# A two-layer decoder trunk on one core: the first four tiles of each transition summed on TensorE from the old residual and y times a diagonal, and six constant products ahead of them

## The reference

```python
def rms_norm(x, g, eps=RMS_EPS):
    xf = x.astype(jnp.float32)
    y = xf * lax.rsqrt(jnp.mean(xf * xf, axis=-1, keepdims=True) + eps)
    return (y * g.astype(jnp.float32)).astype(x.dtype)
...
    h = x
    for i in range(DEPTH):
        hn = rms_norm(h, pre_mix_g[i])
        ...
            y = conformer_conv(hn, ...)      # layer 0
            y = diff_attention(hn, ...)      # layer 1
        h = h + rms_norm(y, post_mix_g[i])
        f = conv_ffn(rms_norm(h, pre_ffn_g[i]), ffn_w_in[i], ffn_w_dw[i], ffn_w_out[i])
        h = h + rms_norm(f, post_ffn_g[i])
        h = h + per_layer_embed(h, p[i], ple_pre_g[i], ple_w_gate[i], ple_b_gate[i],
                                ple_w_proj[i], ple_post_g[i])
    return h
```

## Time and profile before

| | |
|---|---|
| time, median of 3 runs | 2510.29 us (2509.94 to 2512.2) |
| the profiled execution's own time | 2504.14 us |
| its span in the profile | 2502.3 us |
| mean granted TensorE clock | 0.993 of full |
| PE busy | 2430.5 us, 97% of the span |
| DVE busy | 1666.5 us, 67% |
| ACT busy | 1307.0 us, 52% |

### The profile page before, as it was taken

How to read it: one execution, slowest core, us unless ns; L and a number is a source line. 1 busy time by engine, 2 the same in 40 slices (tenths; PEclk the granted TensorE clock), 3 DMA queues, 4 the chain that set the end, 5 groups by cost and what they waited for, 6 DMA issues and landing times.

```text
span 2502.3 us, 40724 instructions
## 1 busy us (share of the span) xinstructions
PE 2430.5 (97%) x12610; PEld 2082.6 (83%) x12610; DVE 1666.5 (67%) x2183; ACT 1307.0 (52%) x1882; POOL 27.6 (1%) x49
## 2 busy tenths in 40 slices
PE   7999899999999999999999999999999999999997
PEld 6888787888888888887788887888888888888876
DVE  5889756777777764446665577567777777544465
ACT  6555545555555544446454455465655656444463
POOL 1000000000000000000000000000000000000000
PEclk9999999999999999999999999999999999999999
DMA  6444254666566665555565543646666666655554
GB/s 212 133 133 135 76 192 153 193 186 188 183 190 194 192 202 194 193 193 200 183 181 188 189 155 128 203 148 191 194 192 187 185 185 198 204 193 194 194 197 138
DMA packets 365325, 448.28 MB, mean 179 GB/s; under 512 B 27084, under 2 KB 273726, under 8 KB 364076
## 3 DMA queue, kind: packets, MB, share of 16 engines
q1 hardware_dynamic: 363452, 436.75, 54.7%
q0 software_dynamic: 1776, 10.41, 1.3%
HBM read 444.95 MB, written 2.10 MB: 179 GB/s over the span
## 4 chain that ended last, share of the span: by engine, by line
PE 88%; issue 5%; DVE 3%; ACT 2%; DMA 1%; DVEq 0%; SPq 0%; POOL 0%; ACTq 0%; POOLq 0%
PE ps L1273 34%; PE ps L1275 17%; PE ps L1308 11%; PE ps L1310 11%; PE ps L1309 11%; PE ps L1346 2%; PE ps L1253 1%; DVE v_conv L935 1%; DMA gain<-in_post_ffn_g 1%; DVE w_lo L808 1%; PE ps L1412 0%; PE ps L1426 0%; DVE h L860 0%; ACT w_hi L503 0%; DVE x L843 0%
## 5 line engine op out<-in xcount | busy, mean ns | idle before, releaser
L808 DVE TENSOR_TENSOR w_lo<-raw,w_hi 128x1024 fp32r<-128x1024 f32 x824 | 1002.4, 1224 | 664.5 <-ACT w_hi L503 635.7
L1273 PE MATMUL ps<-x,w_hi 128*128 128x512 f32 x3840 | 1341.2, 394 | 7.0 <-DVE w_lo L808 3.8
L503 ACT CAST w_hi<-raw 128x1024 fp32r<-128x1024 f32 x824 | 859.4, 1049 | 839.7 <-PE ps L1275 423.4
L1275 PE MATMUL ps<-x,w_lo 128*128 128x256 f32 x3840 | 1073.7, 280 | 0.0
L1273 PEld LDWEIGHTS ps<-x,w_hi 128*128 128x128 f32 x3840 | 718.9, 187 | 169.8 <-DVE w_lo L808 5.0
L1275 PEld LDWEIGHTS ps<-x,w_lo 128*128 128x128 f32 x3840 | 724.9, 189 | 0.6
L1308 PE MATMUL ps<-w_hi,mid 128*128 128x512 f32 x704 | 274.1, 389 | 4.6 <-DVE w_lo L808 4.6
L1310 PE MATMUL ps<-w_hi,mid 128*128 128x512 f32 x704 | 273.9, 389 | 0.0
L1309 PE MATMUL ps<-w_lo,mid 128*128 128x512 f32 x704 | 273.9, 389 | 0.0
L1308 PE MATMUL ps<-w_hi,x 128*128 128x512 f32 x640 | 254.3, 397 | 7.0 <-DVE x L980 3.6
L1309 PE MATMUL ps<-w_lo,x 128*128 128x512 f32 x640 | 250.1, 391 | 0.0
(11 more groups left out here) (144 smaller groups left out, 1213.9 us busy)
## 6 DMA issues: line engine op xcount, KB each, us to landing
raw<-in_ffn_w_in SPq DMA_DIRECT2D x704, 256.0 KB, 3.1
raw<-in_ffn_w_out SPq DMA_DIRECT2D x352, 256.0 KB, 3.0
raw<-in_conv_w_pw SPq DMA_DIRECT2D x192, 256.0 KB, 3.1
raw<-in_attn_w_qkv SPq DMA_DIRECT2D x192, 256.0 KB, 2.9
raw<-in_ple_w_gate SPq DMA_DIRECT2D x128, 256.0 KB, 3.5
raw<-in_attn_w_o SPq DMA_DIRECT2D x64, 256.0 KB, 3.2
raw<-in_ple_w_proj SPq DMA_DIRECT2D x16, 256.0 KB, 3.4
h<-in_x SPq DMA_DIRECT2D x4, 512.0 KB, 5.9
```

What stands on the lines that cost most here:

```text
L503: nc.scalar.copy(w_hi[:, u % RING], raw[:, u % RING]).then_inc(hi_split, 1)
L808: nc.vector.tensor_tensor(w_lo[:, u % RING], raw[:, u % RING], w_hi[:, u % RING].bitcast(F32), ALU.subtract).then_inc(split_done, 1)
L1273: mm(ps[:, 4 * s + f], w_hi[:, u % RING, q, columns], x[:, kt].rearrange("p a t -> p (a t)"), start=kt == 0, stop=False)
L1275: ins = mm(ps[:, 4 * s + f, 0:T], w_lo[:, u % RING, q, columns], x[:, kt, 0], start=False, stop=kt == KT - 1)
```

## The change

The transitions are rebuilt. The gain products write `y` into SBUF (the place of `z`, at the arena's start) and no longer in place, so the eight PSUM banks are free sooner. The first four tiles of x (chunk 0 of h) no longer wait for the residual: PE sums each in PSUM from two ordinary products, old h times the identity and y times `rdiag`, the diagonal of rstd, which DVE makes. The residual for chunk 0 is done last. The other 12 tiles are transposed as before, four at a time, after units 0, 1 and 2 of the next stage. Ahead of the old-h products stand six products of constants (ones times identity, `keep_warm`), whose result nobody reads. The stage may start when two tiles of x are ready, not four (and not eight for the rest). The statistic of y is summed in two steps, with the first three chunks ahead. In the down stages the gains of chunks 0 to 2 are applied in the last chunk. The tile slots in PSUM are now 8 to 15 (banks 4 to 7), each used twice. The spread of the second root comes one unit later in the up stages, after unit 6.

```diff
+            def keep_warm(bank, n):
+                for _ in range(n):
+                    mm(ps[:, bank, 0:P], ones[:], ident[:], start=True, stop=True)
+
+            def first_tiles(add):
+                pe.wait_ge(y_ready, PIECES * ADD[add] + PIECES - HALVES)
+                keep_warm(0, WARM)
+                def whole(kt, half):
+                    mm(tiles[:, turned_at("", kt), P * half:P * (half + 1)], h[:, half, P * kt:P * (kt + 1)], ident[:],
+                       start=True, stop=False)
+                def added(kt, half):
+                    return mm(tiles[:, turned_at("", kt), P * half:P * (half + 1)], y[:, half, P * kt:P * (kt + 1)], rdiag[:, half],
+                              start=False, stop=True)
+                for kt in range(4):
+                    if kt >= 2:
+                        pe.wait_ge(y_ready, PIECES * ADD[add] + PIECES - HALVES + kt - 1)
+                    whole(kt, 0)
+                pe.wait_ge(rdiag_ready, HALVES * (ADD[add] + 1))
+                for kt in range(4):
+                    added(kt, 0)
+                    whole(kt, 1)
+                    added(kt, 1).then_inc(turned, 1)
...
+            def turn_rest(add, left, j):
+                if j < NC - 1:
+                    pe.wait_ge(x_ready, KT * LEFT[left] + 4 * (j + 1))
+                    turn_h(add, j + 1)
...
-                        pe.wait_ge(x_ready, KT * LEFT[left] + max(2 * j + 2, KT // 2))
+                        pe.wait_ge(x_ready, KT * LEFT[left] + max(2 * j + 2, KT // 2 if early else 0))
```

On DVE, `new_h` and the end of `times_gain`:

```diff
+                    if last and half == 0:
+                        dve.wait_ge(stats_done, k + 1)
+                        step.mark(nc.vector.tensor_reduce(ssum[:], stat[:, :, 0:NC - 1], AX_X, ALU.add))
+                        dve.wait_ge(dve_step, step.value())
+                        step.mark(nc.vector.tensor_scalar(ssum[:], ssum[:], 1.0 / D, RMS_EPS, ALU.mult, ALU.add))
                     dve.wait_ge(stats_done, k + (half + 2))
                     if last and half == HALVES - 1:
-                        inverse_root(stat, D)
...
+                        nc.vector.scalar_tensor_tensor(meansq[:], stat[:, :, NC - 1], 1.0 / D, ssum[:],
+                                                       ALU.mult, ALU.add).then_inc(var_ready, 1)
...
                 dve.wait_ge(rstd_ready, stats[0])
-                residual(source, range(PIECES // 2))
-                x_low(left, scale, range(KT // 2))
+                for half in range(HALVES):
+                    nc.vector.tensor_scalar(rdiag[:, half], ident[:], rstd[:, half:half + 1], None, ALU.mult).then_inc(rdiag_ready, 1)
+                dve.wait_ge(y_ready, PIECES * (ADD[add] + 1))
+                residual(UPDATE[0:1])
+                x_low(left, scale, range(0, 2))
+                residual(UPDATE[1:2])
+                x_low(left, scale, range(2, 4))
                 split(None, 0, first + RING - 1, 1)
-                residual(source, range(PIECES // 2, PIECES))
-                x_low(left, scale, range(KT // 2, KT))
-                split(None, 0, first + RING, 2)
+                residual(UPDATE[2:4])
+                x_low(left, scale, range(4, 8))
+                split(None, 0, first + RING, 1)
+                residual(UPDATE[4:6])
+                x_low(left, scale, range(8, 12))
+                dve.wait_ge(turned, KT * (LEFT[left] - (LEFT[left] > LEFT["ln"])) + 4)
+                residual(UPDATE[6:8])
+                split(None, 0, first + RING + 1, 1)
+                x_low(left, scale, range(12, KT))
+                split(None, 0, first + RING + 2, 1)
                 dve.wait_ge(hstats_done, PIECES * (HNORM[left] + 1) + 1)
                 inverse_root(hstat, D)
-                split(None, 0, first + RING + 2, 2)
+                split(None, 0, first + RING + 3, 1)
```

More of the change, by code:

```diff
@@ L313, in trunk, with turned_at @@
         out_stored = sem("out_stored")
+        def turned_at(left, kt):
+            return kt if left in ("mix0", "attn") else KT // 2 + 2 * (kt % 4) + kt // 4 % 2
+        UPDATE = [*range(HALVES, PIECES), *range(HALVES)]
         def used(u):
@@ L514, in col, with h_squares @@
                 return cols[:, bass.ds(k + col_at[name], 1)]
-            def h_squares(norm, add=None, pieces=range(PIECES)):
-                for n in pieces:
-                    c, half, columns = piece(n)
+            def h_squares(norm, add=None, steps=range(PIECES)):
+                for n in steps:
+                    c, half, columns = piece(n if add is None else UPDATE[n])
                     if add is None:
@@ L708, in _ @@
                 act.wait_ge(p_turned, layer + 1)
-                nc.scalar.copy(p_x[:, :, 0], tiles[:, 14:16]).then_inc(p_hi, 1)
+                nc.scalar.copy(p_x[:, :, 0], tiles[:, 8:10]).then_inc(p_hi, 1)
                 keep_rstd((2, 4)[layer])
@@ L858, in residual @@
+                    nc.vector.tensor_tensor(y_rows(c, half), piece_of(half), gain[:, bass.ds(c * UNIT_N, UNIT_N)],
+                                            ALU.mult).then_inc(y_ready, 1)
+            def residual(pieces):
                 for n in pieces:
-                    c, half, columns = piece(n)
-                    nc.vector.scalar_tensor_tensor(h[:, half, columns], source(c, half), rstd[:, half:half + 1],
+                    _, half, columns = piece(n)
+                    nc.vector.scalar_tensor_tensor(h[:, half, columns], y[:, half, columns], rstd[:, half:half + 1],
@@ L1239, in turn @@
                             ins = nc.tensor.transpose(tiles[:, kt, P * half:P * (half + 1)], hn[:, half, P * kt:P * (kt + 1)], ident[:])
[L1240 to L1254 removed]
+                    ins.then_inc(turned, 4)
@@ new lines, in turn_h @@
+            def turn_h(add, c):
+                for half in range(HALVES):
+                    pe.wait_ge(h_updated, PIECES * ADD[add] + HALVES * (c - 1) + half + 1)
+                    for kt in range(4 * c, 4 * c + 4):
+                        ins = nc.tensor.transpose(tiles[:, turned_at("", kt), P * half:P * (half + 1)], h[:, half, P * kt:P * (kt + 1)], ident[:])
+                        if half == HALVES - 1:
+                            ins.then_inc(turned, 1)
+            def turn_rest(add, left, j):
+                if j < NC - 1:
+                    pe.wait_ge(x_ready, KT * LEFT[left] + 4 * (j + 1))
+                    turn_h(add, j + 1)
@@ L1280, in feature_chunk @@
                 early = 0
-                if i is None and n == 0:
+                if i is None and n == 0 and left == "mix0":
                     early = 2
```

120 lines of the change are left out of this document (58 added, 62 removed).

## The result

| | before | changed |
|---|---|---|
| median | 2509.87 us (20 runs, 2504.08 to 2513.39) | 2517.12 us (20 runs, 2508.02 to 2523.01) |
| the profiled execution's own time | 2504.14 us | 2520.8 us |
| span | 2502.3 us | 2518.9 us |
| mean granted clock | 0.993 | 0.995 |

The ratio to the kernel before is 1.0027 (95% 1.0019 to 1.0036): slower by 0.27%, where 2503.2 us was forecast. The scatter belongs to the result: the changed kernel's runs lie 15 us apart, those of before 9.

The account below looks back on a forecast made before the run. PE, busy in 97% of the span, was taken as the bound, its largest wait the transposes for new h (19.3 us). Five transitions 8.0, less 1.1 for clock, plus 0.2: 7.1 us off 2510.29, so 2503.2 (range 2500.5 to 2508.3).

Parts of the forecast that it names:

- the one on the spread: Up stages: spread a unit later; ACT's copy and the second chunk's first split behind it cost about 0.15 us.
- The shorter mean: Ahead of rstd: one short DVE operation replaces two, 0.19 us off each of five transitions and the kernel's end.
- The ten products ahead of rdiag: Constant and old-h products on PE before rstd: 1.8 us of work, free if done before rstd.
- The first product after rstd: Mix0 to ffn0, from rstd to the stage: f32 products at 0.18 us each, stage starts 2.9 us sooner.
- the 1.1 taken: Ple0 to mix1: clock falls; 12 products at half speed cost 0 to 2.2 us, half taken.
- Inside the first chunk: Next stage's first chunk: 24 transposes instead of 16 cost 0.9 us more, plus a 0.1 us wait for low parts.
- an allowance: Each transition: high and low parts each wait for their own tile, bounds 0 and 0.6 us, 0.2 taken.
- 0.2 at the end: End of the kernel, where no transition follows: the statistic's shorter sum takes 0.19 us off.
- (a): DVE and ACT give the gain back inside the stage: each transition gives 0.6 us, so 2507.1; chance 0.19.
- (b): Constant products don't hold PE's clock in the transitions; 5.5 us low everywhere gives 2516; chance 0.13.
- (d): One cover fails: gains delay a split or late bias holds the projection, 2 us each layer: 2507; chance 0.06.

Follow-up runs that it names:

- a_qk4: `a_p4s5` with four constant products added after unit 4 of the qk stage; 2498.11 us (ratio 0.9968), on another chip 2500.94 us (0.9964).
- a_dvecopy: Changed kernel with DVE instead of ACT copying the spread rstd in the up stages; 2502.05 us, ratio 0.9977.
- a_spread5: Changed kernel with the spread back after unit 5 of both up stages, directly behind the embedding rows; 2505.28 us (2496.06 to 2518.37).
- a_p4s5: Changed kernel with embedding rows after unit 4 and spread after unit 5, as in the kernel before; 2501.98 us, ratio 0.9969.
- a_redraw: Changed kernel with one constant product ahead of each chunk of the feature stages' loops; 2527.94 us.
- a_redraw4: `a_p4s5` with four constant products ahead of each chunk of the feature stages' loops; 2550.42 us, one run.
- b_p5s5: Kernel before with embedding rows and spread both after unit 5, in one piece; 2533.77 us.

## Why the prediction was wrong

**The step that failed** is the one on the spread: "In the up stages the spread now comes a unit later, and ACT's copy of it and the first split of the second chunk behind it cost about 0.15." In up0 it cost just that, 0.05 and 0.10 over the pace at two products (428.43 and 428.88). In up1 it cost 1.57 by the same count, 1.30 of it PE's wait, since ACT loads a table there for 1.28 us between the copy and the split. I had walked only through up0's rows. Together that is 1.4 us more than forecast. But most of the price of the wait was never its length: behind it PE went on at the long pace, which costs 9.0 us in each up stage. No term and no rival spoke of that. The sum took each product of the loops as fixed, because neither its code nor its clock changed. The rows to see it were there, in the kernel before: its own pairs run at both paces, changing at interruptions, and I used only means.

**What the medians say.** The mean of the changed kernel's 20 runs, 2516.5, stands some 17 us above the 2499.7 that the profiled one would need without long loops, the qk one among them; in its two profiles three of four up loops were long, and for the other runs this is read from the times. The kernel before has both up loops short in both of its profiles, and never passed 2515.03 in its 98 runs.

**The terms one by one.** The shorter mean: from PE free to POOL's start 2.62 before, 2.42 now, 0.20 for 0.19. The ten products ahead of rdiag cost nothing, as said: the last starts at 398.90, rdiag comes at 399.5. The first product after rstd came 2.47 sooner in mix0 to ffn0, measured from POOL's start, where 2.74 was the forecast (6.47 less 3.73): the f32 product of 128 columns takes 0.222, not 0.18. Tile to tile, three of them, is 0.67 (401.25 to 401.92), and PE's own twelve, not DVE's low part, end last: rdiag's first product at 399.58, the stage at 402.32, 2.74. That is 0.27 in each of five transitions, 1.3 of the sum. The row of the second root had only two of them between other products, 0.36; four in one piece (`a_qk4`) add 0.81 to the row of pairs, so a further one costs 0.22. The 0.08 that two alone seem to save comes back in the pair behind them, which takes 0.43 (422.65 to 423.08 before) instead of 0.35. The Trainium skill, page FP8 and Floating Point Precision, section TensorE Precision Notes, has four passes for true FP32, from which the estimate was 0.23 each and 2.8 for twelve; the trace (0.222, and 2.74 for the twelve) agrees with it and not with my row.

Ahead of the stages the five transitions gave 2.69, 2.67, 1.21, 2.67 and 2.68, 11.9 us in all. In ple0 to mix1 the clock was low for part of the way: 5.85 us from POOL's start, where the variants whose clock held (`a_dvecopy`, `a_spread5`) have 4.39, so 1.46 for the 1.1 taken. This term is a draw of its own: in the 11 profiles of the rebuilt transition it stands between 4.39 and 6.80.

Inside the first chunk the cost was as forecast, 0.9 for the transposes, 0.1 for a wait and 0.2 as an allowance. From the first product of the stage to the last pair of its fifth unit (in the gate stages, to the end of the eighth), the changed kernel takes 1.05, 1.22, 1.11, 1.14 and 1.20 us more than the kernel before, 5.7 in all. In up0 the eight further transposes with the restarts behind their groups are 0.9 of it, as forecast; on top comes a wait of some 0.2 after unit 2, where PE finds x without its low parts 8 to 11: DVE ends them at 412.63, and the transposes that would have started at 412.53 start at 412.69. In the gate stage of layer 0 PE also waited 0.96 us for w_lo at 1186.14, which I had not listed and which the profile of the kernel before does not have.

Together, from the trace: 11.9 - 5.7 - 1.0 + 0.2 at the end = 5.4 us, where the forecast has 7.8 ahead of its 0.15 a transition for later waits (its 7.1 is behind them); the waits at unit 8 (0.15 and 1.57) take another 1.7, which leaves 3.7. The two profiled executions differ by 16.7 us the other way: 21.1 of long pace less 3.7 would be 17.4, and the rest is 1.7 more ahead of the first transition and 2.4 less at the start of the down stages, in waits that also vary between profiles of one kernel.

**The check of that sum** are the versions without long up loops: `a_p4s5` is 7.9 us under its kernel before, `a_dvecopy` 6.0. The mechanism of the transitions was right and its size nearly so. That these medians enclose the forecast's 7.1 is in part luck, since the clock in ple0 to mix1 and the waits of the down stages move a run by some 2 us each. Another step of the change, the later spread, undid it.

**The rivals.** (a), giving it back through DVE and ACT, came closest in form: a wait inside the first chunk. But its price was not in the wait. (Its figure of 2507.1 also leaves out the 1.1 that the sum takes for the clock; with it, it is 2508.2.) (b), the clock, is out: PEclk was 1.00 in four transitions, and without the constant products it was so in three of them. (d), a cover that fails, is there in small. Gain and bias are issued at 1161.14 and 1161.71, about as far behind rdiag as forecast; DVE stood 1.75 us on the bias, and behind it ACT stood 2.73, 0.83 and 1.93 us on the weights of the projection (before, 1.67 once). That the wait of 0.96 us in the gate stage comes of this is likely, but not tested. What stays open is why one interruption leaves the short pace and another the long one. The records show only its pattern (below).

## What to carry to other kernels

Before you price a change by products of unchanged code, look at the interval between their starts, not at the mean of their length, in each stage and on both sides of each interruption; where there are two paces, the last interruption ahead of a long loop can cost many times its own length. A wait of a tenth of a microsecond on a full engine may not be worth a tenth if a loop of a thousand products follows: here one of 0.05 us stood ahead of a loop at the long pace once, and ahead of one at the short pace twice. When runs of a kernel scatter more than those of its predecessor, take that as a finding of its own: count the products of several profiles in the same window before you believe any cause for the median.

## What was not expected of the hardware

- Pairs of 512 and 256 columns with new weights for each run at 0.3467 or 0.3533 us at the same granted clock of 1.00, and keep the one they have: up to 1360 pairs in a row without a change. The products of the token stages (512 columns each) have one pace alone in five profiles compared, 0.227.
- Four transposes (or, in the qk stage of `a_qk4`, four products), eight pairs, and then two f32 products left the short pace in 30 of 30 places in 14 profiles, whatever the pace before, until the next interruption or wait. In 18 of these places nothing interrupted the loop behind, and all 18 loops stayed short; in 8 PE then waited at unit 8 (0.05 to 4.1 us), and 3 of those 8 loops were long, the very same wait of 0.05 us being followed by the long pace once and by the short one twice. (The other 4 are of `a_redraw` and `a_redraw4`.) The same six operations at once left the pace twice long (`b_p5s5`) and twice short (`a_spread5`). A single product ahead of each chunk made it alternate in up0 and stay long in qk and up1; four in each chunk made a cycle of three. What quantity PE carries from one to the other, no view here shows.
